# Input also laid out transposed by the host, un-normalised first projections, roots applied at evictions, first chunks in pieces

## The reference

```python
h = rms_norm(x, norm1_g)          # x * rsqrt(mean(x*x) + EPS) * g, over the 1,024 channels
proj = h @ w_in
(rx, rgate, q, kc, vc, ks, vs, kw, vw, nsa_g, mg_rnn, mg_attn) = jnp.split(proj, splits, axis=-1)
...
qh = rms_norm(heads(q, N_HEADS), q_norm_g)      # over 64 channels of a head
k_cmp = rms_norm(compress(heads(kc, N_KV), ...), k_cmp_norm_g)
v_cmp = compress(heads(vc, N_KV), ...)
k_slc = rms_norm(heads(ks, N_KV), k_slc_norm_g)  # k_win from kw likewise; vs, vw are used as they are
```

## Time and profile before

| | us |
|---|---|
| median of 3 runs | 812.32 (812.21 to 812.46) |
| span of the profiled execution, first to last instruction | 810.6 |
| PE busy | 799.6 (99%) |
| DVE busy | 599.4 (74%) |
| ACT busy | 487.0 (60%) |
| POOL busy | 27.1 (3%) |
| first projection matmul starts at | 10.17 |

### The profile page before, as it was taken

One profiled execution on the slowest core, in us unless ns is written; L12 is line 12 of the kernel. 1 busy time (PEld: TensorE's weight loads), 2 busy tenths in 40 slices (PEclk: granted clock), 3 DMA queues, 4 the chain that ended last, 5 costly groups with the idle time before them and its releaser, 6 DMA issues.

```text
span 810.6 us, 11913 instructions
## 1 busy us (share of the span) xinstructions
PE 799.6 (99%) x4813; PEld 693.2 (86%) x4813; DVE 599.4 (74%) x773; ACT 487.0 (60%) x738; POOL 27.1 (3%) x38
## 2 busy tenths in 40 slices
PE   8999999999999999999999999999999999999996
PEld 7889998888888888988888888888888988888885
DVE  6774698998957986897878778877777665655556
ACT  6555598877757454765666566546755654544552
POOL 1102000000000000000000000020110000000000
PEclk9999999999999999999999999999999999999999
DMA  8446432342434674456455555764453655555441
GB/s 337 164 156 251 170 126 104 118 155 73 151 119 159 229 288 156 156 188 227 160 206 174 201 197 175 256 237 147 146 196 121 211 201 196 174 219 191 161 152 52
DMA packets 22630, 143.79 MB, mean 177 GB/s; under 512 B 2608, under 2 KB 3248, under 8 KB 8240
## 3 DMA queue, kind: packets, MB, share of 16 engines
q1 hardware_dynamic: 20880, 137.72, 48.3%
q10 hardware_dynamic: 1696, 5.31, 1.8%
HBM read 141.97 MB, written 1.05 MB: 176 GB/s over the span
## 4 chain that ended last, share of the span: by engine, by line
PE 93%; ACT 3%; DVE 2%; DMA 1%; issue 1%; DVEq 0%; SPq 0%; ACTq 0%
PE PS L1748 19%; PE PS L1752 10%; PE PS L1801 10%; PE PS L1802 10%; PE PS L1805 10%; PE PS L1735 5%; PE PS L1736 4%; PE PS L1740 4%; PE PS L2115 3%; PE PS L1764 2%; PE PS L2094 2%; PE PS L1858 1%; PE PS L1892 1%; PE PS L2119 1%; PE PS L1869 1%; PE PS L2065 1%
## 5 line engine op out<-in xcount | busy, mean ns | idle before, releaser
L1074 DVE TENSOR_TENSOR WL<-RAW,WH 128x2048 fp32r<-128x2048 f32 (+2 forms) x127 | 285.1, 2247 | 31.1 <-ACT WH L629 31.0
L629 ACT ACTIVATE WH<-RAW 128x2048 fp32r<-128x2048 f32 (+2 forms) x127 | 238.2, 1877 | 47.0 <-PE PS L1805 25.7
L1490 DVE TENSOR_TENSOR HLS<-PS,HLS 128x512 f32<-128x512 f32 x46 | 31.7, 689 | 92.7 <-ACT HLS L977 92.7
L1748 PE MATMUL PS<-CHL,WH 128*128 128x512 f32 x352 | 87.9, 392 | 0.0
L1735 PE MATMUL PS<-BHL,WH 128*126 128x256 f32 (+1 forms) x336 | 83.6, 287 | 0.0
L977 ACT ACTIVATE HLS<-PS 128x512 f32<-128x512 f32 x46 | 27.4, 595 | 90.7 <-PE PS L1752 86.3
L1736 PE MATMUL PS<-BHL,WH 128*126 128x256 f32 (+1 forms) x336 | 81.8, 282 | 0.0
L1748 PE MATMUL PS<-BHL,WH 128*128 128x512 f32 x320 | 79.9, 392 | 0.0
L1748 PEld LDWEIGHTS PS<-CHL,WH 128*128 128x128 f32 x352 | 63.9, 189 | 11.8
L1802 PE MATMUL PS<-WH,AHL 128*128 128x512 f32 x176 | 68.8, 391 | 0.0
L1801 PE MATMUL PS<-WH,AHL 128*128 128x512 f32 x176 | 68.7, 390 | 0.0
(11 more groups left out here) (313 smaller groups left out, 1311.1 us busy)
## 6 DMA issues: line engine op xcount, KB each, us to landing
RAW<-in_w_stream SPq DMA_DIRECT2D x108, 1024.0 KB, 4.8
RAW<-in_w_stream SPq DMA_DIRECT2D x11, 1008.0 KB, 4.9
RAW<-in_w_stream SPq DMA_DIRECT2D x8, 704.0 KB, 4.5
WF<-in_w_stream SPq DMA_DIRECT2D x2, 1024.0 KB, 5.4
LN<-in_ln ACTq DMA_DIRECT2D x2, 1024.0 KB, 5.2
WF<-in_w_stream SPq DMA_DIRECT2D x4, 294.0 KB, 3.6
X<-in_x SPq DMA_DIRECT2D x2, 512.0 KB, 4.2
RAW<-in_w_stream SPq DMA_DIRECT2D x2, 512.0 KB, 6.8
```

The source lines that it names most:

```text
L629: eng.activation(WH[:, c % NSLOT, 0:CHUNKS[c][2]], raw(c), ACT.Copy).then_inc(w_hi, 1)
L1074: eng.tensor_tensor(WL[:, c % NSLOT, 0:CHUNKS[c][2]], raw(c), f32(WH[:, c % NSLOT, 0:CHUNKS[c][2]]), ALU.subtract).then_inc(w_lo, 1)
L1490: eng.tensor_tensor(HLS[:, n % 4, :, :], PS[:, bank:bank + 2, 0:TOK], HLS[:, n % 4, :, :], ALU.add)\
L1748: eng.matmul(PS[:, bank, :], wh, HL[:, k, :, :].rearrange("p a t -> p (a t)"), start=(k == 0), stop=False)
```

## The change

1. The host also gives x transposed with norm1_g before it (`in_xt`, 8 + 2,048 floats a partition). It comes in three DMAs into XTG, two of them from ACT's queue. ACT and DVE make g*x, **not normalised**, into CH and CL from it. The PE transposes, the scaled copies of x and the 14 (now 11) filler matmuls ahead go or shrink.
2. Chunk 0 comes in three DMAs (512, 512, 1,024 columns), chunk 1 in two, and both are split in those pieces.
3. x itself is loaded behind kv chunk 3. Its squares (`x_squares`, on ACT and DVE) and POOL's roots stand behind `split(3)`.
4. V, KSQ and QSQ are scaled by the root in ACT; POOL multiplies the powers of k and q by it (two and one more operations each).
5. For the transposed chunks a normalised x is still wanted: behind kv chunk 3 PE makes the roots as a row in all partitions (RS_BANK, 2 matmuls), DVE multiplies XT by it (8 operations, L1272 of the changed kernel), ACT copies the high half to BH (4, L798), DVE subtracts to BL (4, L1279).
6. `q` 0 and 1 move ahead of `cmp` 0 and 1, and some banks change. (The diff also renames semaphores of the second feed-forward part; nothing moves there.)

```diff
@@ -91,8 +91,9 @@
 def chunk_list():
 
     out = [("kv", i, CHUNK, True) for i in range(4)]
+    out += [("q", i, CHUNK, True) for i in range(2)]
     out += [("cmp", i, CHUNK, True) for i in range(2)]
-    out += [("q", i, CHUNK, True) for i in range(4)]
+    out += [("q", i, CHUNK, True) for i in range(2, 4)]
     out += [("w1", i, CHUNK, False) for i in range(2)]
     out += [("rnn", GATE_TILE, 2 * KD * RP, True)]
     mg = 0
...
-        Q_BANKS = (6, 0)
+        Q_BANKS = (0, 0)
+        CMP_BANKS = (2, 3)
+        KT_BANKS = (4, 6)
+        RS_BANK = 2
...
-            for t in range(NT):
-                eng.dma_start(X0[:, t, :], A_x[t * P:(t + 1) * P, :]).then_inc(x_in[t], 16)
             for c in LOAD_ORDER:
-                if c == 2:
+                if c == 4:
+                    for t in range(NT):
+                        eng.dma_start(X0[:, t, :], A_x[t * P:(t + 1) * P, :]).then_inc(x_in[t], 16)
                     eng.dma_start(CN[:, P:NCONST], A_consts[:, P:NCONST]).then_inc(const_in, 16)
...
+                        for n in range(2):
+                            part = slice(512 * n, 512 * n + 512)
+                            eng.dma_start(raw(c)[:, part], source[:, part]).then_inc(w0_in[n], 16)
+                        eng.dma_start(raw(c)[:, 1024:CHUNK], source[:, 1024:CHUNK]).then_inc(raw_in[slot], 16)
+                        rest = slice(KD + 4 * TOK, KD + KD * TOK)
+                        eng.dma_start(XTG[:, rest], A_xt[:, rest]).then_inc(xt_in[2], 16)
+                    elif c == 1:
+                        eng.dma_start(raw(c)[:, 0:1024], source[:, 0:1024]).then_inc(w1_in, 16)
+                        eng.dma_start(raw(c)[:, 1024:CHUNK], source[:, 1024:CHUNK]).then_inc(raw_in[slot], 16)
...
-                power(krs[:, 8 * b:8 * b + 8], kss[:, 8 * b:8 * b + 8], 8, HD, EPS, k_rstd)
+                power(krs[:, 8 * b:8 * b + 8], kss[:, 8 * b:8 * b + 8], 8, HD, EPS)
+                for t in range(NT):
+                    h = slice(8 * b + 4 * t, 8 * b + 4 * t + 4)
+                    eng.tensor_scalar(krs[:, h], krs[:, h], rsx[:, t:t + 1], None, ALU.mult).then_inc(k_rstd, 1)
             for n in range(2):
...
                         wait_tile(eng, c, t)
-                        eng.activation(V[:, t, br, :], PS[:, 4 + 2 * br + t, 256:512], ACT.Copy)
+                        eng.wait_ge(x_rstd, t + 1)
+                        eng.activation(V[:, t, br, :], PS[:, 4 + 2 * br + t, 256:512], ACT.Copy, scale=rsx[:, t:t + 1])
                         if 2 * br + t >= 2:
                             eng.wait_ge(k_ss, 2 * br + t - 1)
-                        eng.activation(KSQ[:, t, :], PS[:, 4 + 2 * br + t, 0:256], ACT.Square).then_inc(k_sq, 1)
+                        eng.activation(KSQ[:, t, :], PS[:, 4 + 2 * br + t, 0:256], ACT.Square,
+                                       scale=rsx[:, t:t + 1]).then_inc(k_sq, 1)
...
+                if kind == "q" and i == 0:
+                    for kp in range(4):
+                        eng.wait_ge(xt_ready, 2 + kp + 1)
+                        eng.activation(BH[:, 2 * kp:2 * kp + 2, :], XT[:, 2 * kp:2 * kp + 2, :], ACT.Copy).then_inc(xt_hi, 1)
...
             def gained_hi(kp):
-                eng.wait_ge(xt_done, kp + 1)
+                eng.wait_ge(xt_in[min(kp, 2)], 16)
                 for k in (2 * kp, 2 * kp + 1):
-                    last = eng.activation(BH[:, k, :], PS[:, kp, 256 * (k % 2):256 * (k % 2) + TOK], ACT.Copy,
-                                          scale=G1[:, k:k + 1])
+                    last = eng.activation(CH[:, k, :], XT[:, k, :], ACT.Copy, scale=XTG[:, k:k + 1])
...
+            two = KD + 2 * TOK
+            eng.dma_start(XTG[:, 0:two], A_xt[:, 0:two]).then_inc(xt_in[0], 16)
+            eng.dma_start(XTG[:, two:two + 2 * TOK], A_xt[:, two:two + 2 * TOK]).then_inc(xt_in[1], 16)
+            eng.dma_start(CN[:, 0:P], A_consts[:, 0:P]).then_inc(const_in, 16)
+            for n in range(2):
+                part = slice(512 * n, 512 * n + 512)
+                eng.wait_ge(w0_in[n], 16)
+                eng.activation(WH[:, 0, part], raw(0)[:, part], ACT.Copy).then_inc(w_part_hi, 1)
+            gained_hi(1)
+            eng.wait_ge(raw_in[ARRIVAL[0][0]], 16)
+            eng.activation(WH[:, 0, 1024:CHUNK], raw(0)[:, 1024:CHUNK], ACT.Copy).then_inc(w_hi, 1)
             gained_hi(2)
+            eng.wait_ge(w1_in, 16)
+            eng.activation(WH[:, 1, 0:1024], raw(1)[:, 0:1024], ACT.Copy).then_inc(w_part_hi, 1)
             gained_hi(3)
+            eng.wait_ge(raw_in[ARRIVAL[1][0]], 16)
+            eng.activation(WH[:, 1, 1024:CHUNK], raw(1)[:, 1024:CHUNK], ACT.Copy).then_inc(w_hi, 1)
...
+                if c == 1:
+                    x_squares()
...
+                if kind == "q" and i == 0:
+                    eng.wait_ge(chunk_done, c)
+                    for k in range(KD):
+                        ins = eng.scalar_tensor_tensor(XT[:, k, :], XT[:, k, :], XTG[:, k:k + 1], PS[:, RS_BANK, 0:TOK],
+                                                       ALU.mult, ALU.mult)
+                        if k % 2:
+                            ins.then_inc(xt_ready, 1)
+                    for kp in range(4):
+                        eng.wait_ge(xt_hi, 3 + kp + 1)
+                        pair = slice(2 * kp, 2 * kp + 2)
+                        eng.tensor_tensor(BL[:, pair, :], XT[:, pair, :], f32(BH[:, pair, :]), ALU.subtract).then_inc(xt_lo, 1)
...
-                if kind == "q" and i < 2:
-                    n = i
+                if kind == "q" and i >= 2:
+                    n = i - 2
...
+                    eng.scalar_tensor_tensor(CL[:, k, :], XT[:, k, :], XTG[:, k:k + 1], f32(CH[:, k, :]), ALU.mult,
+                                             ALU.subtract).then_inc(xt_lo, 1)
+
+            def first_low(c, part, ready, count, low):
+                eng.wait_ge(ready, count)
+                eng.tensor_tensor(WL[:, c, part], raw(c)[:, part], f32(WH[:, c, part]), ALU.subtract).then_inc(low, 1)
+
+            def x_squares():
+                for t in range(NT):
+                    eng.wait_ge(x_in[t], 16)
+                    eng.scalar_tensor_tensor(XN[:, t, 512:DM], X0[:, t, 512:DM], 1.0 / DM, X0[:, t, 512:DM], ALU.mult, ALU.mult,
+                                             accum_out=ssx[:, 2 * t + 1:2 * t + 2]).then_inc(x_sq2, 1)
+                eng.wait_ge(const_in, 48)
+                for t in range(NT):
+                    eng.wait_ge(x_rstd, t + 1)
+                    eng.tensor_scalar(DG[:, t, :], ident, rsx[:, t:t + 1], None, ALU.mult).then_inc(dg_ready, 1)
...
+            eng.wait_ge(xt_in[0], 16)
+            for k in range(2):
+                eng.tensor_scalar(CH[:, k, :], XT[:, k, :], XTG[:, k:k + 1], None, ALU.mult).then_inc(xt_ready, 1)
+            first_low(0, slice(0, 512), w_part_hi, 1, w_part_lo)
+            first_low(0, slice(512, 1024), w_part_hi, 2, w_part_lo)
+            gained_lo(0)
+            first_low(0, slice(1024, CHUNK), w_hi, 1, w_lo)
+            gained_lo(1)
+            first_low(1, slice(0, 1024), w_part_hi, 3, w_part_lo)
             gained_lo(2)
+            first_low(1, slice(1024, CHUNK), w_hi, 2, w_lo)
...
-                        last = t_half(c, (b, b + 1), i, BH, BL)
+                        last = t_half(c, (b, b + 1), i, CH, CL)
+                    if i == 3:
+                        eng.wait_ge(dg_ready, NT)
+                        for t in range(NT):
+                            last = eng.matmul(PS[:, RS_BANK, P * t:P * t + P], WARM[:, :], DG[:, t, :], start=True, stop=True)
                 if kind == "cmp":
-                    m = MB_NO[c]
-                    bank = mb_bank(m)
+                    bank = CMP_BANKS[i]
+                    eng.wait_ge(xt_lo, KD + 4)
                     for j in range(2):
                         last = f_tile(PS[:, bank, 256 * j:256 * j + 256], c, 1024 * j, P, BH, BL)
                 if kind == "q":
                     b = Q_BANKS[i // 2]
-                    if i == 0:
-                        eng.wait_ge(kn_ready, 2 * NT)
-                        eng.wait_ge(k_sq, 2 * NT)
                     if i == 2:
-                        eng.wait_ge(mb_act, 2)
-                    last = t_half(c, (b, b + 1), i, BH, BL)
+                        eng.wait_ge(kn_ready, 3 * NT)
+                    last = t_half(c, (b, b + 1), i, CH, CL)
...
-            for _ in range(14):
+            eng.wait_ge(fills_ready, 1)
+            for _ in range(11):
                 eng.matmul(PS[:, 4, 0:P], WARM[:, :], WARM[:, :], start=True, stop=True)
```

More of the change, by code:

```diff
@@ L568, in _, with power @@
             used = [0]
-            def power(out, ss, n, mean_of, eps, ready):
+            def power(out, ss, n, mean_of, eps, ready=None):
                 t = tmp[0:out.shape[0], used[0]:used[0] + n]
@@ L574, in power @@
                 link(eng.tensor_scalar(t, ss, 1.0 / mean_of, eps, ALU.mult, ALU.add))
```

(17 more changed lines are left out.)

170 lines of the change are left out of this document (74 added, 96 removed).

## The result

| | before | changed |
|---|---|---|
| median | 812.30 us (812.21 to 812.46) | 820.03 us (819.68 to 820.32) |
| profiled execution: own time, span | not given apart, 810.6 | 819.85, 818.1 |
| ratio | | 1.0095 (1.0083 to 1.0106) |
| first projection matmul | 10.17 | 5.85 |
| first matmul of cmp 0 | 32.04 | 47.97 |

The change costs 7.7 us. The forecast, 816.8, has the sign and is 3.2 us short; its range ended at 819.6.

A forecast was written before the change was run, and what follows sets the result against it. PE, busy 799.6 of 810.6 us, was taken as the bound. Waiting at cmp 0 for DVE's queue makes it 3.1 us later and the slow clock adds 1.4: 812.3 + 4.5 = 816.8 us, range 813.0 to 819.6.

The forecast's parts named there:

- The mechanism: At cmp 0's first matmul PE waits 5.5 us for DVE's BL, then runs at half clock; DVE almost never idle.
- Kv 3's landing, 16.9: Start of DVE's queue: kv 3's weights land at 16.9 us, as 455 KB fewer lie ahead than at 17.99 before.
- For the pieces I take no loss in the DMA engines: First loads: splitting them into smaller pieces was priced at nothing.
- The roots: Queue from kv 3's low half (21.1) through squares, POOL's roots and powers and two 0.30 multiplies to first KN's end, 29.0.
- PE is through at 40.5: PE's work ahead of cmp 0 ends at 40.5 us, against 42.9 before: 2.4 us gained were nothing in the way.
- The clock, 1.4: Behind the wait at cmp 0: 3.4 us at the slow pace, 0.179 against 0.107 a matmul, lose PE 1.4 us.
- Nothing swallows the 3.1: After cmp 0 PE is at 99%, so its 3.1 us later resumption stays in the total.
- Behind it the order is the old one: After cmp 0 the order of work is as before the change; no further loss was priced there.
- Rival 4: More is late: kv 3's landing slips through smaller pieces, or the slow clock lasts twice as long; 817.7 to 820; chance 0.10.
- Rival 2: At cmp 0 DVE keeps up and the early start is kept: PE gains 2.4 us, time 809.9; chance 0.08.
- Q 2 waits for QN, whose chain ... has two whole cmp chunks as cover: Behind cmp: QN's chain starts when q 1 is through and is covered by two cmp chunks, so no loss.

The follow-up runs named there:

- e3: Changed kernel with DVE's XT and BL operations put ahead of the second KN and chunk 6's low half, and ACT's BH copies earlier: 815.94 us.
- e2: Changed kernel plus forty idle 128-column matmuls on PE in front of the wait at cmp 0: 821.67 us.
- e11: Changed kernel with e3's order, second KN behind chunk 6's low half, fifteen small DVE operations behind the last query work, and e9's roots and V: 810.71 us.
- e5: Changed kernel plus 24 idle 128-column matmuls on PE in front of the wait at cmp 0: 818.00 us.
- e9: Changed kernel with keys and queries squared un-normalised, POOL adding scaled epsilon instead of multiplying roots, and V evicted behind KSQ: 818.96 us.
- e1: Changed kernel with cmp's products reading un-normalised x, so without the wait for the normalised operand: 820.48 us.

## What held in the prediction, and which terms failed

The mechanism is as forecast; the sum is not. Three terms were too small, and together they put the time above the range: the operand's arrival, which hangs on kv 3's landing ("16.9"), the price of the slow clock ("1.4"), and the stretch behind the wait, which was put at nothing.

- **The mechanism held.** One wait of 5.4 at the first matmul of cmp 0, where 5.5 was foretold, ended by DVE's BL; the half clock behind it; DVE, from 22 us on, idle mainly behind POOL. e3 shows that the place in the queue was the reason: the same operations, put earlier, end 7.1 us sooner.
- **"Kv 3's landing, 16.9"** was short by 1.2 (18.13). This is the largest single miss. "For the pieces I take no loss in the DMA engines" had no row for it (the earlier trace rows has two loads of 229 and 226 KB, but no price of a piece); with the long pieces the landing is 17.10 and 16.82, so the 16.9 was right for whole loads, and the pieces are what failed. (Among the profiles with short pieces the changed kernel's is the second latest.)
- **The roots.** From the low half of kv 3 (22.37, 1.3 late) to the first KN (29.70, 1.9 late) 0.6 more was lost, in small parts: POOL has both roots of x 3.2 behind the low half for 2.95, the scaled V and KSQ take 0.48 and 0.47 in place of 0.38, DVE waits 2.75 in place of 2.66. POOL's two multiplications took 0.59, as forecast (0.30 each). Everything behind that, 29.70 to 47.83, took 18.1 as the sum had it (27.8 to 45.9). So the operand came 1.9 late, and PE at 47.97, not 46.05.
- **"PE is through at 40.5"** was short by the same 1.9 (42.5): first product 5.85 for 5.1, kv 0 and 1 done at 19.0 for 17.7, q 0's low half 0.9 late for 0.7. Of the early start of 4.3 us only 0.5 was left there, where the forecast had 2.4. Both sides of the wait slid together, which is why its length was right and its place wrong. That they slid by the same amount is in part luck: only the late landings are common to both.
- **"The clock, 1.4"** measured 1.7 to 1.8 in the changed kernel (30.85 from cmp 0 to W0, for 29.11 in e2 and 29.01 in e11), 2.0 by e5's median, and 2.6 in e9. The slow stretch was not 3.4 us of work but 4, and the pace was misread: the two windows of the earlier trace rows count matmuls that reach in from outside, so 0.179 and 0.107 are too short. The fillers' starts are 0.213 apart at first and 0.11 later, by which 3.4 us would have cost 1.6; those of cmp 0's matmuls are 0.213 and 0.12 apart. And the earlier trace rows read a granted clock of 1.00 at both paces, so no row there shows that the slow pace of the fillers was the clock; the 0.51 of this kernel does.
- **"Nothing swallows the 3.1"** held, and 0.6 came on top behind W0 (span behind its start 738.7 before, 739.3 in the changed kernel, 738.6 in e9): the 0.3 at W0's low-half products and the 0.4 at 172 us that e9 takes away. "Behind it the order is the old one" priced them at nothing. DVE's queue is the later there too.
- 1.9 (place of cmp 0) + 0.4 (clock) + 0.6 (behind W0) = 3.0 of the 3.2 in the profiled execution; the median lies another 0.2 above that execution.
- **The rivals.** Rival 4 had the right things in it, a late landing and a longer slow clock, and 0.10 was too little for it: the chain's terms had been read short, one after the other, and none long to make up for it. Rival 2's 809.9, and the 812 that e1 was given, took for granted that PE meets DVE's queue nowhere behind cmp 0. "Q 2 waits for QN, whose chain ... has two whole cmp chunks as cover" holds for the changed kernel, where PE is late itself; with the wait taken away (e1) q 2 waits 0.9 and W0 4.0, and the time is not 809.9 or 812 but 820.5.

What the idea is worth, its new work placed well: 812.3 - 810.7 = 1.6 us, out of an early start of 4.3.

## What to carry to other kernels

When an operation moves onto an in-order engine that already feeds the bound engine, write down that engine's whole queue up to the last place where the bound engine meets it, not to the first: the first wait hides the others, and taking it away alone can win nothing. Look for small work with late readers standing in front of work with an early one; here the order was worth 4.1 us, and the fifteen small operations 5.3 in the version that had lost its first wait. And price a stall twice, as idle time and as slow time behind it.
